# Two-stream modulation vectors of the first blocks: formed on VectorE instead of TensorE

## What is computed

```python
s_lat = jax.nn.silu(c)
s_ctx = jax.nn.silu(c_ctx)
for layer in range(DEPTH):
    shift, scale, gate = jnp.split(s_lat @ w_mod[layer] + b_mod[layer], 3, axis=-1)
    shift_c, scale_c, gate_c = jnp.split(s_ctx @ w_mod[layer] + b_mod[layer], 3, axis=-1)
    x_in = x * (1.0 + scale[:, None, :]) + shift[:, None, :]
    ...
    x = _post_norm(x, gate[:, None, :] * y, ln_g[layer], ln_b[layer])
...
for l in range(DEPTH):
    shift, scale, gate = jnp.split(c_act @ w_ada[l] + b_ada[l], 3, axis=-1)
```

## Time and profile before

| | |
|---|---|
| median of 3 runs | 2838.55 us (2832.22 to 2839.12) |
| the profiled execution's own time | 2837.41 us |
| its span on the engines | 2835.6 us |
| PE busy | 2697.0 us, 95% |
| POOL busy | 1663.2 us, 59% |
| DVE busy | 1648.7 us, 58% |
| ACT busy | 1197.5 us, 42% |
| DMA | 599.09 MB, 211 GB/s over the span |

### The profile page before, as it was taken

One profiled execution on the slowest core, in us unless ns is written; L12 is line 12 of the kernel. 1 busy time (PEld: TensorE's weight loads), 2 busy tenths in 40 slices (PEclk: granted clock), 3 DMA queues, 4 the chain that ended last, 5 costly groups with the idle time before them and its releaser, 6 DMA issues.

```text
span 2835.6 us, 49284 instructions
## 1 busy us (share of the span) xinstructions
PE 2697.0 (95%) x21319; PEld 2458.9 (87%) x21319; DVE 1648.7 (58%) x1907; ACT 1197.5 (42%) x1406; POOL 1663.2 (59%) x875
## 2 busy tenths in 40 slices
PE   5799999999999999999999969999999899999999
PEld 3489988888889999978999958999889889998799
DVE  2344444553444657686676655764776557646763
ACT  0233444333333334334567354633454355434452
POOL 0057777997778799888556803064578450456520
PEclk8699999999999999999999979999999999999999
DMA  9999998998888997767555835665567756655565
GB/s 338 283 314 265 266 265 253 276 289 243 242 241 231 279 276 229 210 203 212 161 150 159 233 100 178 166 177 142 168 182 216 195 158 167 175 142 164 169 183 154
DMA packets 842265, 599.09 MB, mean 211 GB/s; under 512 B 22071, under 2 KB 764865, under 8 KB 841537
## 3 DMA queue, kind: packets, MB, share of 16 engines
q1 hardware_dynamic: 838224, 582.83, 71.1%
q10 hardware_dynamic: 3824, 13.11, 1.2%
HBM read 589.46 MB, written 6.29 MB: 210 GB/s over the span
## 4 chain that ended last, share of the span: by engine, by line
PE 77%; DVE 8%; DMA 6%; POOL 5%; ACT 2%; SPq 1%; issue 1%; DVEq 0%; POOLq 0%; ACTq 0%
PE G L2393 53%; PE G L2412 4%; DMA ring<-in_w_mod_dram 3%; POOL ring L828 3%; PE A L2350 2%; DVE ring_r L1470 2%; POOL mod_rows L836 1%; DMA const<-in_w_mod_dram 1%; PE A L2477 1%; PE A L2483 1%; POOL ring L835 1%; PE A L2480 1%; PE A L2661 1%; PE G L2499 1%; PE G L2642 1%
## 5 line engine op out<-in xcount | busy, mean ns | idle before, releaser
L828 POOL TENSOR_SCALAR ring<-ring,act_in 128x512 f32<-128x512 f32 x448 | 961.7, 2158 | 1024.7 <-DMA ring<-in_w_ada_dram 798.3
L2393 PE MATMUL G<-H_r,ring_r 128*128 128x256 f32 x9008 | 1496.5, 286 | 35.0 <-DVE S_r L1459 19.2
L2393 PEld LDWEIGHTS G<-H_r,ring_r 128*128 128x128 f32 x9008 | 1307.8, 191 | 60.6 <-issue 42.0
L1470 DVE TENSOR_TENSOR ring_r<-ring,ring_r 128x2048 fp32r<-128x2048 f32 x346 | 825.3, 2387 | 280.3 <-ACT ring_r L869 279.2
L869 ACT ACTIVATE ring_r<-ring 128x2048 fp32r<-128x2048 f32 x346 | 661.9, 1913 | 373.7 <-PE G L2393 81.0
L2393 PE MATMUL G<-M_r,ring_r 128*128 128x256 f32 x4464 | 773.0, 284 | 0.0
L2393 PEld LDWEIGHTS G<-M_r,ring_r 128*128 128x128 f32 x4464 | 635.0, 191 | 9.4 <-issue 8.6
L2393 PE MATMUL G<-S_r,ring_r 128*128 128x256 f32 x1536 | 437.5, 285 | 0.0
L836 POOL TENSOR_TENSOR mod_rows<-mod_rows,ring 128x512 f32<-128x512 f32 x196 | 331.4, 1691 | 15.4
L835 POOL TENSOR_TENSOR ring<-ring 128x512 f32<-128x512 f32 x196 | 325.1, 1659 | 16.3
L2393 PEld LDWEIGHTS G<-S_r,ring_r 128*128 128x128 f32 x1536 | 296.1, 193 | 0.1
(11 more groups left out here) (446 smaller groups left out, 2634.7 us busy)
## 6 DMA issues: line engine op xcount, KB each, us to landing
ring<-in_w_in_dram SPq DMA_DIRECT2D x120, 1024.0 KB, 5.5
ring<-in_a_w_in_dram SPq DMA_DIRECT2D x98, 1024.0 KB, 6.9
ring<-in_w_ada_dram SPq DMA_DIRECT2D x192, 512.0 KB, 6.3
const<-in_w_mod_dram SPq DMA_DIRECT2D x192, 256.0 KB, 5.4
ring<-in_c_w_in_dram SPq DMA_DIRECT2D x48, 1024.0 KB, 5.8
ring<-in_w_mod_dram SPq DMA_DIRECT2D x16, 2048.0 KB, 18.0
ring<-in_a_w_out_dram SPq DMA_DIRECT2D x32, 1024.0 KB, 6.2
ring<-in_w_out_dram SPq DMA_DIRECT2D x32, 1024.0 KB, 6.1
```

The costliest lines, as they stand in the source:

```text
L828: g.mark(pool.tensor_scalar(w[:, i, :], w[:, i, :], act_in[:, k, c:c + 1], None, ALU.mult))
L1470: v.tensor_tensor(w_low(tl), w_raw(tl), w_up(tl).bitcast(F32), ALU.subtract).then_inc(w_lo, 1)
L2393: ins = pe.matmul(G[tl.bank][:, 0:SEQ], w, x, start=(k == 0 and n_ == 0), stop=(k == KT - 1 and n_ == 2))
```

## The change

PE no longer touches the 24 two-stream blocks' weights. For a unit m, DVE takes each of its two 128 x 256 pieces and, for each of the two streams, multiplies it by that stream's per-partition factor and adds it to a running sum in `const` (`gemv_part`; the very first piece of a block by `tensor_scalar`, the rest by `scalar_tensor_tensor`). So a unit is 4 DVE instructions. Per block, PE turns the four 128 x 128 pieces of the two sums with four transposes into `A[3]`, DVE adds along the free axis with one `tensor_reduce`, and `mod_store` follows as before. ACT's copy is gone.

The units are laid out evenly: two a tile, tile m // 2 + 2 for unit m, from q = 2 to q = 97. DVE executes the first right behind `lower` and the second behind the odd steps of the chain. SP loads units 2(q - 3) and 2(q - 3) + 1 at tile q, with the same three slots; the wait for unit m - 3 is now one for DVE's two counts `gemv_sum`. POOL's units keep their places. The scaling of the first norm's factors (`fold_norm`), which needs the last block, moves from ahead of `ac_out` to its ninth tile.

```diff
 def gemv_units_by(q):
-    begin = [10 + 11 * n // 3 for n in range(GEMV_BLOCKS + 1)]
-    return sum(min(8, max(0, -(-8 * (q + 1 - a) // (b - a)))) for a, b in zip(begin, begin[1:]))
+    return min(GEMV_UNITS, max(0, 2 * (q - GEMV_FIRST)))
...
-GEMV_TILE, POOL_TILE = unit_tiles(gemv_units_by, GEMV_UNITS), unit_tiles(pool_units_by, POOL_UNITS)
+POOL_TILE = unit_tiles(pool_units_by, POOL_UNITS)
+GEMV_COLS_AT = {gemv_tile(8 * _n + 7) + 1: _n for _n in range(GEMV_BLOCKS)}
...
                 if m >= 3:
-                    sp.wait_ge(gemv_used, m - 2)
+                    for i in range(2):
+                        sp.wait_ge(gemv_sum[i], 2 * (m - 2))
                 sp.dma_start(gemv_unit(m), mod_w[l][:, k:k + 2, j * BW:(j + 1) * BW]).then_inc(gemv_full[m % 3], 16)
...
-                    mod_store(*MOD_BLOCKS[n], three(G[(q - 1) % 2], BW), 2, gemv_out)
+                    V(v.tensor_reduce(cols[:, 40:44], A[3][:, :].rearrange("p (t x) -> p t x", x=P), AX.X, ALU.add))
+                    mod_store(*MOD_BLOCKS[n], cols[:, 40:44].rearrange("p (t i) -> p t i", i=2), 2, gemv_out)
...
+            def gemv_part(q, u):
+
+                m = 2 * (q - GEMV_FIRST) + u
+                if 0 <= m < GEMV_UNITS:
+                    n, w = m // 8, gemv_unit(m)
+                    v.wait_ge(gemv_full[m % 3], 16 * (m // 3 + 1))
+                    if m % 8 == 0 and n:
+                        v.wait_ge(gemv_cols, n)
+                    for x in range(2):
+                        k = 2 * (m % 8) + x
+                        for i in range(2):
+                            a = act_in[:, k, i:i + 1]
+                            if k == 0:
+                                ins = v.tensor_scalar(gemv_sums[:, i, :], w[:, x, :], a, None, ALU.mult)
+                            else:
+                                v.wait_ge(gemv_sum[i], KT * n + k)
+                                ins = v.scalar_tensor_tensor(out=gemv_sums[:, i, :], in0=w[:, x, :], scalar=a,
+                                                             in1=gemv_sums[:, i, :], op0=ALU.mult, op1=ALU.add)
+                            ins.then_inc(gemv_sum[i], 1)
...
                     chain.upto(2 * j)
                     lower(q0 + j + LEAD)
+                    gemv_part(q0 + j, 0)
                     chain.upto(2 * j + 1)
+                    gemv_part(q0 + j, 1)
...
-                    for i in range(2):
-                        k = 2 * u + i
-                        o = 32 * (k % 4)
-                        ins = pe.matmul(A[3][o:o + 32, 0:BW], act_all[:, 3 * k:3 * k + 32], gemv_unit(m)[:, i, :],
-                                        start=(k < 4), stop=(k >= KT - 4), skip_group_check=True)
-                    ins.then_inc(gemv_used, 1)
...
+                    for t in range(2):
+                        for i in range(2):
+                            c = 2 * t + i
+                            ins = pe.transpose(A[3][:, c * P:(c + 1) * P], gemv_sums[:, i, t * P:(t + 1) * P], ident)
+                    ins.then_inc(gemv_cols, 1)
```

More of the change, by code:

```diff
@@ L122, in unit_tiles @@
     return tiles
-GEMV_TILE, POOL_TILE = unit_tiles(gemv_units_by, GEMV_UNITS), unit_tiles(pool_units_by, POOL_UNITS)
[L126 to L130, removed]
+POOL_TILE = unit_tiles(pool_units_by, POOL_UNITS)
+GEMV_COLS_AT = {gemv_tile(8 * _n + 7) + 1: _n for _n in range(GEMV_BLOCKS)}
+MOD_COLS_AT = {}
 for _p in range(len(POOL_BLOCKS)):
@@ L531, in build @@
         late_in = sem("late_in")
-        gemv_used, gemv_rows, gemv_cols, gemv_out = sem("gemv_used"), sem("gemv_rows"), sem("gemv_cols"), sem("gemv_out")
+        gemv_cols, gemv_out = sem("gemv_cols"), sem("gemv_out")
+        gemv_sum = [sem(f"gemv_sum{i}") for i in range(2)]
         pool_used, pool_cols, pool_out = sem("pool_used"), sem("pool_cols"), sem("pool_out")
@@ L905, in _ @@
             upper(1)
[L907 to L912, removed]
             def load_back(i):
@@ L1704, in pairs, with fold_norm @@
                 return mod[:, at:at + 2 * KT].rearrange("p (k i) -> p k i", i=2)
[L1706 to L1711, removed]
+            def fold_norm():
+                v.wait_ge(gemv_out, GEMV_BLOCKS)
+                V.mark(v.tensor_tensor(pairs(0), pairs(MOD_AT[1] + 2 * KT), both("ln_g"), ALU.mult))
+                V(v.tensor_tensor(pairs(2 * KT), pairs(MOD_AT[1] + 2 * KT), both("ln_b"), ALU.mult))
+                V(v.tensor_tensor(pairs(2 * KT), pairs(2 * KT), pairs(MOD_AT[1]), ALU.add))
+                for name in ("ln_g", "ln_b"):
+                    at = ROWS[name][0]
+                    V(v.tensor_scalar(pcol[:, at:at + KT], pcol[:, at:at + KT], ALPHA, None, ALU.mult))
             for phase, x, s, chain in (("ac_out", XH, 1, Pace(turn_y())), ("ax_out", X256, 0, Pace(norm(0, XH, H_hi)))):
@@ L1720, in _ @@
                     mod_event(FIRST[phase][0] + j)
+                    if phase == "ac_out" and j == 8:
+                        fold_norm()
                     chain.upto(2 * j + 1)
@@ L2335, in _ @@
                         ins.then_inc(x_t, 1)
[L2337 to L2346, removed]
-                    for i in range(2):
-                        k = 2 * u + i
-                        o = 32 * (k % 4)
-                        ins = pe.matmul(A[3][o:o + 32, 0:BW], act_all[:, 3 * k:3 * k + 32], gemv_unit(m)[:, i, :],
-                                        start=(k < 4), stop=(k >= KT - 4), skip_group_check=True)
-                    ins.then_inc(gemv_used, 1)
             def after_first_half(q):
                 if q in GEMV_COLS_AT:
[L2357 to L2361, removed]
+                    n = GEMV_COLS_AT[q]
+                    for i in range(2):
+                        pe.wait_ge(gemv_sum[i], KT * (n + 1))
+                    if n == 0:
+                        pe.wait_ge(first_used, SHIFT_SCALE)
+                    else:
+                        pe.wait_ge(gemv_out, n)
+                    for t in range(2):
+                        for i in range(2):
+                            c = 2 * t + i
+                            ins = pe.transpose(A[3][:, c * P:(c + 1) * P], gemv_sums[:, i, t * P:(t + 1) * P], ident)
+                    ins.then_inc(gemv_cols, 1)
                 if q - 1 in MOD_COLS_AT:
```

16 lines of the change are left out of this document (7 added, 9 removed).

## The result

| | before | after |
|---|---|---|
| median | 2835.39 us (4 runs) | 3518.14 us (3507.37 to 3518.96, 4 runs) |
| ratio | | 1.2402, 95% interval 1.2367 to 1.2437 |
| span of the profiled execution | 2835.6 us | 3517.2 us |
| PE / DVE / ACT / POOL busy | 2697.0 / 1648.7 / 1197.5 / 1663.2 us | 2781.6 / 1915.8 / 1185.1 / 1506.1 us |
| DMA | 599.09 MB, 211 GB/s | 599.07 MB, 170 GB/s |

The account below looks back on a forecast made before the run. PE bounds the kernel at 8.7 us a tile; the change makes a 15.0 us load loop: 143.9 + 1425 + 50 + 54 + 20 - 8 = 1685 us for tile 99 instead of 985.0, +700 us, 3540 us (3340 to 3700).

Parts of the forecast that it names:

- The loop: SP, ACT and DVE, tiles 5 to 99: next weight tile issued only after landing, rounding, lowering, one unit's sums; chance 0.80.
- lowering: DVE's `lower` of a weight tile after ACT's rounding, inside each turn: 2.40 us.
- plain turn: One tile's pass through load, rounding, lowering, sums and issue: 15.0 us against 8.7 before; 95 turns make 1425 us.
- The landing: Weight tile's transfer from SP's issue to arrival, in each turn: taken as 7.6 us, with bounds 5.6 and 8.0 us.
- from the last sum to the weight tile's issue: SP, from DVE's count to issuing the weight tile: one unit and POOL's unit, 0.9 us a turn.
- The long turns: 16 turns with heads' weights on SP add 50 us, 16 with exponentials before `lower` 54 us, six alike 20 us.
- short turns: Four turns with no POOL unit yet to load ahead of the weight tile: 8 us less.
- the later phases: After tile 99 no unit is loaded and waits stay as before: no added cost.
- The markers: Expected signs between first tile and `ac_out`: stretch length, PE's busy share, DMA rate, granted clock, who waits for whom.
- GpSimd and VectorE in each other's way: Rival, first 98 tiles: contention slows POOL, SP waits for it, 207 us, about 3045 us; chance 0.08.
- The faster case: Rival: DVE sums early enough that SP never waits long, PE gains, about -75 us, 2765 us; chance 0.04.
- PE's clock: Rival, first 98 tiles: PE's clock falls and PE sets a slower pace, 16 us a tile, 3640 us; chance 0.06.

Follow-up runs that it names:

- corrected kernels: Units loaded one tile later than in the change; the one quoted at 0.94 also had POOL's operations on 2 of 512 columns: 2826.53 us.

## Why the prediction was right

**The loop.** Its place, its members and its count were as forecast: ACT waited 95 times for a weight tile, the chain of work that ended last runs through the turns as listed, and issuing the units one tile later, with all work unchanged, took back 558 of 683 us. A wait for the lowering added to the kernel before cost 540 us, though there partly by way of PE's own late units.

**Its size.** Forecast 15.0 us a plain turn, measured 14.76. The landing was 7.9 at the median for an assumed 7.6, lowering 2.33 for 2.40, a sum 0.482 for 0.486, and from the last sum to the weight tile's issue 0.6 passed (538.27 to 538.87) for 0.9. The transfer was the one unknown with a wide bound, and the row nearest in what stood ahead of it (8.0 us) was nearer than the median over the stretch (6.8).

**The long turns.** A turn with both a head's weights ahead of its tile and that head's exponentials ahead of the lowering lasted from 490.27 to 509.47, 19.2 us; in it the transfer took 9.37 us, and from the end of the rounding to the lowering 3.0 passed, for 3.4. The head's two issues stand at the end of the turn before, 15.7 us (474.56 to 490.27). The two turns together are 5.4 us longer than two plain ones, where the terms said 3.1 + 3.4 = 6.5. The forecast took the two kinds of long turn for different turns; that they fall together changes nothing in the sum.

**Two errors that offset each other.** Tile 99's low part was ready earlier than forecast:

```profile
1653.39 2.55 DVE L1465 TENSOR_TENSOR ring_r<-ring,ring_r 128x2048 fp32r<-128x2048 f32 x1 [6.96 <-ACT ring_r L873]
```

1655.9 us, for 1685. Over all 95 turns the mean was (1655.9 - 143.8) / 95 = 15.9 us against 16.2. Of the 29 us, 95 x 0.24 = 23 are the plain turn; what the long and short turns add over the plain one came to 110 us for 116. The other way, PE began tile 99 only at 1665.9, 10 us after its low part was ready: it had waited 15.71 us at the transposes ahead of it for DVE's last sum, and the forecast had that wait at nothing. So the start of tile 99, 681 us late for 700, fits better than the loop's own time does, and that much of the fit is luck. The transposes themselves took 22.4 us (L2372), while the small step that they replace took 12.1; the forecast took the two for equal.

**What came behind.** Costing the later phases at nothing held: tile 99 was 681 us late, the end 683 us.

**The markers.** The stretch was to be about 1550 us long, with 140 to 150 GB/s: 1540 us and 146. PE was to be busy for little over half: 61%. SP was to wait over 1000 us at the units: 1029. One marker was off. I expected PE to wait for `lower` in nearly every tile; it waited there 14 times, and 21 times at the transposes, which come first in its order.

**The rivals.** GpSimd and VectorE in each other's way: wrong for this change, and right in part for the kernel with later loads, where POOL's work costs some 88 us. In the change itself POOL's unit was done before DVE's sums, as argued: 712 of the 720 sums ran with POOL idle. Had every sum paid the mean of 0.709 us, the time would have been 3625 us; a sum took 0.482 us. The faster case fell with the order on DVE. PE's clock did drop (last section), and the loop's slack absorbed it.

## What to carry to other kernels

A queue that issues the loads of several consumers is a thread like any engine: before a wait in it is moved to another engine, write down what that engine has in front of the event, and whether one of the queue's own next transfers is among it. Here the buffers (four raw slots) were all there, and a wait of one unit, placed one tile too early, made one slot of them usable; moving it one tile took back four fifths of the loss. And work taken from a full engine is only a gain if the engine that gets it can deliver at the time at which the first one asks: DVE had about half of its time idle on paper, and with the loads one tile later PE still waited for its sums 104.7 us.

## What the runs showed of the hardware that was not expected

- The granted clock of PE follows the turn of the loop. Stretches of 7 us of the kernel after:

```profile
505.00:512.00 7.00, 1.86 (x9) 1.89 (x10) 5.74 (x11) 0.00 (x0) 0.00 (x0) 0.50 0.30 95
...
526.00:533.00 7.00, 7.00 (x68) 6.70 (x66) 0.87 (x2) 0.96 (x1) 4.94 (x4) 1.00 0.81 242
```

  In the first, after 17.5 us without a product, PE ran at 0.50 (1.2 GHz); in the second, busy throughout, at 1.00 (2.4 GHz). Over the stretch the clock was 0.78 where it was 0.99, and PE was busy 932 us for less work than the 837 us before. Hardly any of it was on the chain: the tiles' products (L2404) are 1.0% of it in this stretch. In the corrected kernels, a lower granted clock goes with longer busy time for the same products (589 to 613 us at 0.94, above). "TensorE: Matmul & The Clock Gate" of the Trainium skill (section HAM oscillation) describes bursts that start slow after each wait for a transfer; the trace agrees, though PE here waited for DVE's sums, which waited for a transfer.
- The slowing between GpSimd and VectorE depends on whether their instructions meet, not on how busy GpSimd is. One and the same sum took 0.482 us with POOL busy 33% of the stretch but idle during nearly every sum, 0.690 with POOL busy 41% of it where the order on SP made them meet (0.905 in the turn shown), 0.642 with POOL busy 65%, and 0.486 with POOL's work cut. "GPSIMD Engine Reference" of the Trainium skill (section Key points) names this contention without a price; here a sum takes a third longer in the mean, and nearly twice as long where they meet.
